# Two transformer blocks on one core: the order of the matmuls in 512-column products, at the seams, and in the latent attention

## The reference, cut to what matters

```
x = x + ab_mixer(rms_norm(x))            # mLSTM heads + spatial gating, weights 1024 wide
x = x + relu(rms_norm(x) @ w1)**2 @ w2   # feed-forward 0, width 4096
x = x + mla_mixer(rms_norm(x))           # latent attention: h @ w_in -> (cq, ckv, kr);
                                         #   q = rms_norm(cq) @ w_uq; k, v = rms_norm(ckv) @ w_ukv
x = x + relu(rms_norm(x) @ w1)**2 @ w2   # feed-forward 1
x = rms_norm(x)
x = x + rms_norm(chunk_attention(rms_norm(x)) )                      # second block
x = x + rms_norm((silu(h @ w_gate) * (h @ w_up)) @ w_down), h = rms_norm(x)   # width 2816
```

## Time and profile before

| | |
|---|---|
| Time before, median of 3 | 895.15 us (894.41 to 895.58) |
| Profiled execution, its own time | 894.42 us |
| Its span in the profile | 892.6 us |
| PE busy | 877.9 us, 98% of the span |
| DVE, ACT, POOL busy | 617.4, 441.2, 80.2 us |
| Granted TensorE clock | 0.999 of full speed over the span |

### The profile page before, as it was taken

The page is one execution under the profiler, slowest core; times in us unless marked ns, Lnnn a source line. Parts: engine busy times, 40 slices in busy tenths (PEclk is TensorE's granted clock), DMA queues, the critical chain, the costliest instruction groups (busy, mean ns, idle before and its releaser), DMA issues.

```text
span 892.6 us, 12512 instructions
## 1 busy us (share of the span) xinstructions
PE 877.9 (98%) x4898; PEld 748.0 (84%) x4898; DVE 617.4 (69%) x781; ACT 441.2 (49%) x586; POOL 80.2 (9%) x114
## 2 busy tenths in 40 slices
PE   9999999999999999999999999999999999999997
PEld 8988888888888877778888888879987888888886
DVE  6999777666666668857666666665775676676674
ACT  5795544433333577745333333374555644434432
POOL 3663110000000030011000000010000200000000
PEclk9999999999999999999999999999999999999999
DMA  9764445655554361375555555537333446555541
GB/s 296 246 211 151 147 148 200 213 190 189 188 188 170 108 206 54 100 252 196 200 190 190 191 190 197 189 125 240 131 135 95 142 144 233 189 185 191 188 142 48
DMA packets 97818, 155.87 MB, mean 175 GB/s; under 512 B 4079, under 2 KB 72332, under 8 KB 97772
## 3 DMA queue, kind: packets, MB, share of 16 engines
q1 hardware_dynamic: 95068, 149.37, 49.7%
q0 software_dynamic: 1648, 5.80, 2.1%
q10 hardware_dynamic: 1056, 0.07, 0.1%
HBM read 153.62 MB, written 1.09 MB: 173 GB/s over the span
## 4 chain that ended last, share of the span: by engine, by line
PE 87%; DVE 6%; ACT 3%; SPq 1%; issue 1%; POOL 1%; DMA 1%; DVEq 0%; POOLq 0%; ACTq 0%
PE psum L1963 20%; PE psum L1882 17%; PE psum L1884 16%; PE psum L1883 16%; PE psum L1965 10%; DVE w_lo L1231 2%; PE psum L2370 1%; ACT w_hi L755 1%; DVE h_both L1256 1%; PE psum L2400 1%; ACT h_both L784 1%; PE psum L2476 1%; SPq L517 1%; PE psum L2383 1%; PE psum L1903 1%
## 5 line engine op out<-in xcount | busy, mean ns | idle before, releaser
L1231 DVE TENSOR_TENSOR w_lo<-raw,w_hi 128x2048 fp32r<-128x2048 f32 (+3 forms) x116 | 260.3, 2251 | 93.8 <-ACT w_hi L755 50.0
L1963 PE MATMUL psum<-h_both,w_hi 128*128 128x512 f32 x784 | 278.5, 398 | 0.0
L1965 PE MATMUL psum<-h_both,w_lo 128*128 128x256 f32 x784 | 220.0, 281 | 0.0
L1963 PEld LDWEIGHTS psum<-h_both,w_hi 128*128 128x128 f32 x784 | 147.3, 188 | 36.3 <-DVE w_lo L1231 0.3
L1965 PEld LDWEIGHTS psum<-h_both,w_lo 128*128 128x128 f32 x784 | 148.0, 189 | 1.4
L755 ACT ACTIVATE w_hi<-raw 128x2048 fp32r<-128x2048 f32 (+2 forms) x71 | 129.6, 1837 | 35.6 <-PE psum L1884 33.9
L1882 PE MATMUL psum<-w_hi,g_hi 128*128 128x512 f32 x368 | 145.0, 394 | 0.7 <-DVE g_lo L1840 0.4
L1883 PE MATMUL psum<-w_lo,g_hi 128*128 128x512 f32 x368 | 143.6, 390 | 0.0
L1884 PE MATMUL psum<-w_hi,g_lo 128*128 128x512 f32 x368 | 143.5, 390 | 0.0
L773 ACT ACTIVATE w_hi<-raw 128x2048 fp32r<-128x2048 f32 x66 | 125.9, 1910 | 24.9 <-PE psum L1884 24.9
L940 ACT ACTIVATE g_hi<-g_mul 128x512 fp32r<-128x512 f32 x32 | 20.2, 633 | 171.0 <-DVE g_mul L1544 171.0
(11 more groups left out here) (275 smaller groups left out, 1082.5 us busy)
## 6 DMA issues: line engine op xcount, KB each, us to landing
raw<-in_ffn_w SPq DMA_DIRECT2D x64, 1024.0 KB, 5.3
raw<-in_w_qkv SPq DMA_DIRECT2D x12, 1024.0 KB, 5.2
raw<-in_ab_w_in SPq DMA_DIRECT2D x11, 1024.0 KB, 6.2
raw<-in_w_gate SPq DMA_DIRECT2D x11, 1024.0 KB, 5.4
raw<-in_w_up SPq DMA_DIRECT2D x11, 1024.0 KB, 5.4
raw<-in_w_down SPq DMA_DIRECT2D x11, 1024.0 KB, 5.6
raw<-in_ab_w_out SPq DMA_DIRECT2D x4, 1024.0 KB, 4.9
raw<-in_c_w_out SPq DMA_DIRECT2D x4, 1024.0 KB, 5.7
```

Source lines behind the costliest of these rows:

```text
L1231: ins = dve.tensor_tensor(dst, src, high, ALU.subtract)
L1963: pe.matmul(bank(b + f), wh[:, k, cs], h_both[:, k, :, :].rearrange("p u s -> p (u s)"), start=k == 0, stop=False, skip_group_check=True)
L1965: ins = pe.matmul(bank(b + f)[:, 0:S], wl[:, k, cs], h_hi[:, k, :], start=False, stop=k == KB - 1, skip_group_check=True)
```

## The change

`stationary_both` now issues, for each half f, the 8 matmuls of 512 columns and then the 8 of 256. At the four seams the two terms with the high input come first, after a wait for `h_hi` alone, and the term with the low input after a wait for `h_lo`; the first feed-forward product goes to bank 0 instead of bank 4, and `latent_in` first waits for the third residual, which empties its bank. In the latent attention POOL makes each `q_scale` right behind its own two rms, ScalarE rounds the first w_ukv piece ahead of the first `q_out`, and the wait for queries 7 moves from head step 9 to 11. The tables of feed-forward 0 are done in two parts, behind chunks 2 and 3. In the last gated chunk the up product is one of `stationary_both`, and its multiplication, rounding and subtraction are done in halves of 256 columns, each waited for apart.

```diff
@@ pool
-            for name in ("c0", "c1", "ckv0", "cq0", "ckv1", "cq1"):
+            for name in ("c0", "c1"):
                 rms(name)
             for tb in range(TB):
+                rms(f"ckv{tb}")
+                rms(f"cq{tb}")
@@ act
+            hi(P_UQ + RING)
             q_out(0)
-            hi(P_UQ + RING)
@@ act, glu_chunk
+                if isinstance(c, int) and c == GC - 2:
+                    for f in range(2):
+                        cs = slice(f * S, (f + 1) * S)
+                        act.wait_ge(mul_out, hb + GC + f)
+                        act.activation(g_hi[:, (j + 1) % 2, cs], g_mul[:, (j + 1) % 2, cs], ACT.Copy)\
+                            .then_inc(g_hi_ready, 1)
+                    return
@@ dve, ffn
-                if between:
-                    between()
                 for c in range(1, FC):
...
+                    if between and c in (2, 3):
+                        between[c - 2]()
@@ dve
+            def mul_block(r, f, n_up):
+                if f == 0:
+                    dve.wait_ge(up_half, 1)
+                else:
+                    dve.wait_ge(piece_used, n_up + 1)
+                cs = slice(f * S, (f + 1) * S)
+                dve.tensor_reduce(g_mul[:, r, cs], sums_of(6)[:, f], AX.X, ALU.add).then_inc(up_in, 1)
+                dve.wait_ge(up_in, GC - 1 + f)
+                if f == 0:
+                    dve.wait_ge(act_out, GC)
+                dve.tensor_tensor(g_mul[:, r, cs], g_act[:, r, cs], g_mul[:, r, cs], ALU.mult).then_inc(mul_out, 1)
+            def lo_block(r, f):
+                cs = slice(f * S, (f + 1) * S)
+                dve.wait_ge(g_hi_ready, hb + GC + f)
+                dve.tensor_tensor(g_lo[:, r, cs], g_mul[:, r, cs], g_hi[:, r, cs], ALU.subtract)\
+                    .then_inc(g_lo_ready, 1)
@@ dve, glu_chunk
-                    mul_plain(c + 1, n + 1 + 6 * i)
-                else:
-                    glu_mul(c + 1, r, n + 1 + 6 * i)
+                    mul_block(r, 0, n + 1 + 6 * i)
+                    lo_block(r, 0)
+                    mul_block(r, 1, n + 1 + 6 * i)
+                    lo_block(r, 1)
+                    return
+                glu_mul(c + 1, r, n + 1 + 6 * i)
@@ pe, stationary_both
                     for k in range(KB):
                         pe.matmul(bank(b + f), wh[:, k, cs], h_both[:, k, :, :].rearrange("p u s -> p (u s)"),
                                   start=k == 0, stop=False, skip_group_check=True)
+                    for k in range(KB):
                         ins = pe.matmul(bank(b + f)[:, 0:S], wl[:, k, cs], h_hi[:, k, :],
                                         start=False, stop=k == KB - 1, skip_group_check=True)
+                    if f == 0 and half_done is not None:
+                        ins.then_inc(half_done, 1)
@@ pe, stationary_seam (latent_in and moving_slice alike)
                 for q in range(KB // 2):
+                    h_hi_wait(t, 2 * q)
+                    for f in range(2):
+                        for k in (2 * q, 2 * q + 1):
+                            at = bank(b)[:, f * S:(f + 1) * S]
+                            pe.matmul(at, wh[:, k, f * P:(f + 1) * P], h_hi[:, k, :], start=k == 0 and f == 0,
+                                      stop=False, skip_group_check=True)
+                            pe.matmul(at, wl[:, k, f * P:(f + 1) * P], h_hi[:, k, :], start=False, stop=False,
+                                      skip_group_check=True)
                     h_wait(t, 2 * q)
                     for f in range(2):
                         for k in (2 * q, 2 * q + 1):
-                            ins = product(bank(b)[:, f * S:(f + 1) * S],
-                                          (wh[:, k, f * P:(f + 1) * P], wl[:, k, f * P:(f + 1) * P]),
-                                          h_block(k), k == 0 and f == 0, k == KB - 1, True)
+                            ins = pe.matmul(bank(b)[:, f * S:(f + 1) * S], wh[:, k, f * P:(f + 1) * P], h_lo[:, k, :],
+                                            start=False, stop=k == KB - 1, skip_group_check=True)
@@ pe, latent stage
             split(P_CIN)
+            pe.wait_ge(x_ready, X_AT["c"] + 3)
@@ pe, c_fill
                 if i == 9:
                     qf_wait(6)
+                if i == 11:
                     qf_wait(7)
@@ pe, out_last_two
-                ready()
-                out_block(act_of, n_slot, 0, False, True).then_inc(acc_part, 1)
+                for k in range(2):
+                    ready(k)
+                    wh = w_hi[:, n_slot, :].rearrange("p (k c) -> p k c", k=2)
+                    wl = w_lo[:, n_slot, :].rearrange("p (k c) -> p k c", k=2)
+                    for h in range(2):
+                        cs = slice(h * 512, (h + 1) * 512)
+                        ins = product(bank(h), act_of(k, 0), (wh[:, k, cs], wl[:, k, cs]), False, k == 1)
+                ins.then_inc(acc_part, 1)
@@ pe, gate_up
-                if isinstance(c, int) and c == GC - 1:
-                    stationary((n0 + 1) % RING, T_GLU, 6)
-                else:
-                    stationary_both((n0 + 1) % RING, 6)
+                stationary_both((n0 + 1) % RING, 6, up_half if isinstance(c, int) and c == GC - 1 else None)
```

More of the change, by code:

```diff
@@ L372, in build @@
         up_in = sem("up_in")
+        up_half = sem("up_half")
         g_hi_ready = sem("g_hi_ready")
@@ L1491, in _, with rel_table @@
             lo(P_AOUT + RING)
-            def tables():
+            def rel_table():
                 dve.wait_ge(rel_loaded, 16)
@@ L1501, in tables, with angles @@
                     .then_inc(rel_built, 1)
+            def angles():
                 dve.wait_ge(pos_loaded, 16)
@@ L1933, in h_wait, with h_hi_wait, high_terms, low_term @@
                 pe.wait_ge(h_lo_ready, t_base(t) + PAIRS[t].index(k // 2) + 1)
+            def h_hi_wait(t, k):
+                pe.wait_ge(h_hi_ready, t_base(t) + PAIRS[t].index(k // 2) + 1)
+            def high_terms(dst, stat, mov, first, shared=False):
+                pe.matmul(dst, stat[0], mov[0], start=first, stop=False, skip_group_check=shared)
+                pe.matmul(dst, stat[0], mov[1], start=False, stop=False, skip_group_check=shared)
+            def low_term(dst, stat, mov, last, shared=False):
+                return pe.matmul(dst, stat[1], mov[0], start=False, stop=last, skip_group_check=shared)
             def stationary_slice(slot, t, b, i, between=None, first_use=False):
@@ L1991, in moving_slice @@
                 tb = i // 2
+                ks = (2 * (i % 2), 2 * (i % 2) + 1)
                 if t is not None and tb == 0:
-                    h_wait(t, 4 * j + 2 * (i % 2))
-                for k in (2 * (i % 2), 2 * (i % 2) + 1):
-                    ins = product(bank(banks[tb]), h_block(4 * (j if half is None else half) + k, tb),
-                                  (wh[:, k, :], wl[:, k, :]), j == 0 and k == 0, j == 1 and k == 3)
+                    h_hi_wait(t, 4 * j + ks[0])
+                    for k in ks:
+                        high_terms(bank(banks[tb]), h_block(4 * j + k, tb), (wh[:, k, :], wl[:, k, :]),
+                                   j == 0 and k == 0)
+                    h_wait(t, 4 * j + ks[0])
+                    for k in ks:
+                        ins = low_term(bank(banks[tb]), h_block(4 * j + k, tb), (wh[:, k, :], wl[:, k, :]),
+                                       j == 1 and k == 3)
+                else:
+                    for k in ks:
+                        ins = product(bank(banks[tb]), h_block(4 * (j if half is None else half) + k, tb),
+                                      (wh[:, k, :], wl[:, k, :]), j == 0 and k == 0, j == 1 and k == 3)
                 if i == 3:
@@ L2273, in latent_in @@
                 wh, wl = part(w_hi, n, k1 - k0), part(w_lo, n, k1 - k0)
+                outs = ((0, 0, Q_LORA), (1, Q_LORA, C_IN))
+                if tb == 0:
+                    for ks in (((0, 1), (2,)), ((3,), (4, 5)), ((6, 7),))[j]:
+                        h_hi_wait(T_C, ks[0])
+                        for k in ks:
+                            for b, c0, c1 in outs:
+                                high_terms(bank(b)[:, 0:c1 - c0], h_block(k, 0),
+                                           (wh[:, k - k0, c0:c1], wl[:, k - k0, c0:c1]), k == 0)
+                        h_wait(T_C, ks[0])
+                        for k in ks:
+                            for b, c0, c1 in outs:
+                                ins = low_term(bank(b)[:, 0:c1 - c0], h_block(k, 0),
+                                               (wh[:, k - k0, c0:c1], wl[:, k - k0, c0:c1]), k == KB - 1)
+                    return ins
                 for k in range(k0, k1):
-                    if j == 1 and tb == 1 and k == k0 + 1:
+                    if j == 1 and k == k0 + 1:
                         turn_latent(0, 0, 3)
-                    if tb == 0:
-                        h_wait(T_C, k)
```

(4 more changed lines are left out.)

10 lines of the change are left out of this document (5 added, 5 removed).

## The result

Before: 895.12 us, median of 4 (894.41 to 895.58). After: 884.30 us, median of 4 (884.13 to 885.27). Ratio 0.9882, 95% interval 0.9865 to 0.9899: 10.8 us faster. The prediction was 884.7.

A forecast was written before the change was run, and what follows sets the result against it. PE, busy 98% of the span, was taken as the bound, so only matmul stream cost and PE's waits matter. Terms summed to -10.1 us from the profiled 894.42, giving 884.3, adjusted toward the median to 884.7; range 882.0 to 889.5.

The forecast's parts named there:

- Part A: Feed-forward and gated pieces: eight 512-column matmuls then eight 256s save 0.085 us a piece over 49 pieces; -3.9 us.
- Rival 1: stationary_both pieces: the order of matmul sizes is worth nothing, giving 888.6 us; chance 0.16.
- rival 3: Runs of 256-column matmuls: weight loads come into the open and slow the kernel to 939 us; chance 0.03.
- Part B: Seams: high-input products first hide the low part, so all six PE waits go; -3.2 us.
- Part C: Latent attention: earlier w_ukv rounding removes PE's waits for the kv low part and behind the rope; -2.0 us.
- chain through ScalarE: Latent attention: w_ukv rounding in ScalarE's idle 3.85 us ahead of q_scale readies the kv low part near 327 us.
- Part D: Latent attention heads: waiting for queries 7 two heads later removes PE's 0.9 us wait; -1.1 us.
- Part E: Feed-forward 0: moving the tables to chunks 2 and 3 removes PE's wait for weights behind them; -0.5 us.
- Part F: Last gated chunk: doing the up product's VectorE steps in halves is a loss; +0.6 us.
- no earlier: Last gated chunk: PE starts on its first half at about 878.3 us, against 878.33 with the old three steps.
- some 0.3: Last gated chunk: PE waits twice for g_lo, the second wait some 0.3 us idle.
- Rival 2: Latent attention and feed-forward seams: waits move on instead of going, likely 2.5 us, giving 887.2 us; chance 0.13.

The follow-up runs named there:

- a_turns: Changed kernel with the 512- and 256-column matmuls of every stationary_both piece alternating again one by one; median 889.07 us.
- c_pool: Changed kernel with only GpSimd's latent-attention order as before (four root mean squares, then both q_scale), ScalarE's new order kept; median 884.92 us.
- c_act: Changed kernel with only ScalarE's latent-attention order as before (first queries, then rounding of w_ukv), GpSimd's new order kept; median 885.35 us.
- de_old: Changed kernel with queries 7 waited for at step 9 again and both tables in one piece behind chunk 0; median 887.55 us.
- the fours: Changed kernel with 512- and 256-column matmuls of a piece in alternating runs of four instead of eight; median 886.22 us.
- c_both: Changed kernel with both ScalarE's and GpSimd's latent-attention orders as before; median 886.39 us.

## Why the prediction was right

The sum was right, and nearly every term; in parts A and E errors cancelled, and those two were right partly by luck. Against the stretches:

- **Part A**, -3.9 predicted, -3.85 measured by undoing it. The working held to the distances: 0.233 us for the first 512 behind 256s, 0.227 after five, and 0.113 instead of 0.120 for the first 256. Inside the term two sizes were off and cancelled. In a_turns and after, the 37 pieces that start behind 512s differ by 0.081 us (0.085 was taken); 13 start behind 256s (12 in before), not 9, and differ by 0.063 us and by another 0.036 in the 512s behind them (0.055 was taken). That makes 4.3 us; after loses 0.19 of it to its new wait at the second gated chunk and 0.13 to longer waits for `g_lo`, and a_turns happens to be 0.17 shorter ahead of the first seam, where the two kernels are alike. Rival 1 (order worth nothing, 888.6) fell, as did rival 3: weight loads stay at 186 to 192 ns and eights of 256 columns start every 0.120. The rule of the Trainium skill, "TensorE: Matmul & The Clock Gate", section "Back-to-back issue gap" (columns by the clock and a fixed gap), gives all four orders of sizes one time; the runs show 5.64, 5.59, 5.56 and 5.54 us. The prediction left out that this section of the Trainium skill calls it the gap of an isolated matmul. For a stream of weight loads and matmuls the same section of the Trainium skill gives some 131 ns at 512 columns; the trace differs, a settled stream of 512s goes at 227 here, and the measurement decides.
- **Part B**, -3.2 predicted, -3.05 in the stretch and -3.2 at the four seams measured. All six waits went, and pricing a wait at its idle time and 0.25 us more came out within 5% over the six.
- **Part C**, -2.0 predicted, -2.01 measured. The prediction's sentence that it does not hang on GpSimd's order was right (c_pool), but its chain through ScalarE was only half of it: GpSimd's order alone is enough too (c_act). The two are spare for one another.
- **Part D**, -1.1 predicted, -1.15 by the distance at its wait; neither scores nor maxima were late behind it.
- **Part E**, -0.5 predicted. In before, the distance at 141.45 us was 0.45 over the usual, and that went. But undone in the changed kernel it costs 1.08. The prediction's term was right in the sum only because parts B and E were made together: without E, some 0.6 us of what PE gains up to there goes back to the tables, as de_old shows (B alone was not run). No part of the prediction looked at this.
- **Part F**, +0.6 predicted, +0.50 measured by undoing it. From the end of VectorE's weight subtraction to PE's start it takes 868.45 - 866.33 = 2.12 us, where before took 2.13, "no earlier" as predicted; the first wait shows 0.57 idle and no longer 0.41 because the shorter up piece (5.59 for 5.76) brings PE there 0.17 sooner. The second has 0.36, where "some 0.3" was said.

Undone one by one, the parts make 3.85 + 3.05 + 2.01 + 2.23 - 0.50 = 10.6 us, against 10.0 for all: the 0.6 between them is, by its size, the share of the tables (1.08 - 0.45) that is counted under B and under E. Rival 2 (waits move on, 887.2) left a trace of 0.2 us, the new wait at the second gated chunk. The last 0.8 us of the 10.8 between the medians are not in the stretch of the profiled executions, and their cause stays open; the start of a run varies by more than that, and of before there is one profile only.

## What to carry to other kernels

When one engine is busy 98% of the time, look at what its instructions cost beside each other before looking at its waits: matmuls of two sizes in turn cost 5 ns a pair more than in runs of eight, and over 784 pairs that was over a third of the gain. Where two terms of a product are ready early and one late, issue the early ones first; but check what is next late behind the wait that goes, as the tables were here. For a wait at the end of a chain, look at what is queued in front of its steps: one swap on an idle ScalarE gave 1.33 us, more than the 0.50 that cutting the work in halves had cost.

## What the runs showed of the hardware that was not expected

- The price of a change of matmul size is paid over several matmuls, not at once: behind a run of 256 columns, 512s start 233, 236, 228, 232 and 231 ns apart and then 227; behind a run of 512s, 256s start 113 and 119 and then 120 ns apart. Long runs cost 227 and 120, which is 13 ns over columns by the granted clock (0.998 to 0.999 of 2.4 GHz) for both sizes.
- No simple rule gives the price, and what causes it stays open. A fixed 19 ns for each turn (a change up and one down) fits the fours (+1.9 us, measured +2.0) but not the strict turns: 14 turns a piece more would be 0.27 us, and a piece took 0.08 more. Position behind a change alone does not give it either: in fours the fourth 512 of a run took 233 ns in one run of a piece and 224 in another.
- A GpSimd `q_scale` of one column took 1.89 us in c_both (318.29 to 320.18), where VectorE's weight subtraction ran from 318.38 to 320.13, and 0.31 us in after, where VectorE was at short operations of 0.2 us. GpSimd ends 0.05 us behind the subtraction, as if it had stood behind it. The same pairing gives 1.89 us in before and in c_pool. That agrees with the Trainium skill, "SBUF — State Buffer", section "SBUF: two separate sides": a VectorE operation with two inputs in SBUF and a GpSimd operation that reads SBUF shut one another out for the whole instruction. By that section of the Trainium skill the one that starts first goes first; GpSimd's row starts 0.09 us ahead of the subtraction's and yet ends last, and the rows do not show why.
- Whole executions of one kernel differed by up to 2.1 us (de_old), while the two traces of after agree within 0.1 us from the 201st matmul to the last.
